# Local attention in two stacked transformer blocks: the exponentials of each block of queries are issued one round behind its scores instead of four blocks at once

## The chip, the cores and the metric

The kernel runs on one core of a Trainium2 chip. The metric is the device time of one execution in microseconds. Three runs of the kernel before took 3441.42, 3444.75 and 3445.19 us, a median of 3444.75. The profiled execution took 3442.09 us.

## The reference

512 tokens of width 1024 pass through two stacks of two layers each, in float32. The parts with local attention are two. The first stack's mixer (once per layer) projects the input to a short convolution, to attention with 8 query heads and 2 key heads of 64, and to a gated 31-tap convolution. The second stack's second layer has attention with 16 query heads and 4 key heads. Around them stand feed-forward parts, a recurrent mixer and cross attention, which the change does not touch.

```python
scores = jnp.where(valid, scores, -1e30)          # 128 queries against 3 (or 2) blocks of 128 keys
m = jnp.maximum(jnp.max(scores, axis=-1), sink)
p = jnp.exp(scores - m[..., None])
denom = jnp.sum(p, axis=-1) + jnp.exp(sink - m)
o = einsum(p, v) / denom
```

## The kernel before, in words

Each engine runs its own program, in order. One Python walk (class `Walk`) is run once for each engine, and each engine's class overrides the `p_...` methods that it takes part in. So the order of the walk is the order of every queue. Waits are semaphore waits for named results.

**Projections.** All large products are computed on TensorE in three passes over a high and a low part. A unit is one block of 128 output columns: its weights are loaded, ScalarE makes the high part (`wh`, L1901), VectorE the low part (`wl`, L2124), up to four units ahead, and TensorE runs 8 steps of three products (L1719, L1720, L1727).

**Fillers.** Attention does not run by itself. It is a generator, and `tick` (called after each step of a projection) takes it one round on for every 2.8 steps in the first mixer and every 2 steps in the second stack's attention, after a delay of 8 and 4 steps. In the first mixer each round also advances the long convolution (`long_conv`: two, later four taps on VectorE, L2299) and the removal of the mean from the residual (`center`, L2173 and L2178). At the end of the projections the rounds that are left run without projection steps between them.

**A round of attention** (`attention`). Round n works on the score of block n of a list of heads times 4 blocks of queries, and on earlier ones with fixed lags:

- norm of block n-5: P times 1/denominator (on ScalarE, L1984, in the first mixer; on VectorE, L2292, in the second attention). For block 0 of a head VectorE first adds the sums and inverts them (L2287, L2289).
- value product of block n-9 on TensorE (L1788). After block 3 the head's output is split: high half on ScalarE (L1907), low half on VectorE (L2128), and only then is its bank free.
- score of block n: product on TensorE (L1773), mask, and row maximum on VectorE (L2275).
- turn of block n-7: transposes on TensorE (L1780), copy on ScalarE (L1991).
- in every fourth round, at its end: `exps` of the head. VectorE makes minus the maximum with the sink for 4 blocks in one operation on 4 columns (L2280). ScalarE waits for it, then computes the sink term (L1976) and the four exponentials in place, each with its row sums (L1978).

**Around it** on ScalarE stand the four part copies of each rope (L1971, VectorE goes on with L2260, L2262 and L2268), the sigmoid of a gate (L1996) and plain copies (L1917). A function of another table set has an ACT_TABLE_LOAD ahead of it; copies need none. In a first mixer rounds 0 and 1 are issued before the first gate's sigmoid; in the second attention rounds 0 and 1 are issued before a rope, and there each unit of weights is followed by four rounds.

Of the kernel before, what the change touches and what calls it, by code (L numbers as in the profile page):

```python
# [10 lines left out]
ALU = mybir.AluOpType  # L11
ACT = mybir.ActivationFunctionType
AX = mybir.AxisListType.X

P = 128
# [3 lines left out]
NB = 4  # L19
# [290 lines left out]
class Walk:  # L310
# [497 lines left out]

    def attention(self, heads, H, blocks, mask, sink, outs, done, on_act=False):
        S, C, PT, obank = {}, {}, {}, {}  # L810
        NORM, TURN, VALUE = 5, 7, 9
        a = self.uid("att")

        def score(h, b):
            q, k, v, tile, p0, qk, vk, n = heads[h]
            k0, nk, c0 = blocks(b)
            if b == 0:
                C[h] = self.sm_ring.take()
            bank, f = self.psum.take()
            s, sf = self.tmp.take()  # L820
            self.p_score(f"{a}.{h}.{b}", bank, s, C[h][0], b, nk * P, q[:, b * P:(b + 1) * P],
                         k[:, k0 * P:(k0 + nk) * P], mask[:, c0:c0 + nk * P], (f, qk), (sf, C[h][1]))
            self.psum.give(bank, f"{a}.{h}.{b}.max")
            S[h, b] = s

        def exps(h):
            tiles = [(S[h, b][:, 0:blocks(b)[1] * P]) for b in range(NB)]
            self.p_exps(f"{a}.{h}", C[h][0], tiles, sink(heads[h][-1]), f"{a}.{h}.{NB - 1}.max")

        def norm(h, b):  # L830
            s = S[h, b]
            self.p_norm(f"{a}.{h}", b, C[h][0], s[:, 0:blocks(b)[1] * P], on_act)
            if b == NB - 1:
                self.sm_ring.give(C[h][0], [f"{a}.{h}.{i}.norm" for i in range(NB)])

        def turn(h, b):
            w = blocks(b)[1] * P
            s = S.pop((h, b))
            bank, f = self.psum.take()
            pt, pf = self.tmp.take()  # L840
            k = f"{a}.{h}.{b}"
            self.p_turn(k, bank, s, pt, w, f, pf)
            self.tmp.give(s, f"{k}.turn")
            self.psum.give(bank, f"{k}.pt")
            PT[h, b] = pt

        def value(h, b):
            q, k, v, tile, p0, qk, vk, n = heads[h]
            k0, nk, c0 = blocks(b)
            pt = PT.pop((h, b))  # L850
            if b == 0:
                obank[h] = self.psum.take()
            bank, f = obank[h]
            key = f"{a}.{h}.{b}"
            self.p_value(key, bank[:, b * P:(b + 1) * P], [v(k0 + i) for i in range(nk)], pt, (f, vk[0][vk[1]]))
            self.tmp.give(pt, f"{key}.value")
            if b == NB - 1:
                self.psum.give(bank, outs(tile, p0, bank, f"{key}.value"))
            done[0] = f"{key}.value"

        for n in range(H * NB + VALUE):
            while n < H * NB and len(heads) <= n // NB:
                yield
            for lag, f in ((NORM, norm), (VALUE, value), (0, score), (TURN, turn)):
                if 0 <= n - lag < H * NB:
                    f(*divmod(n - lag, NB))
            if n < H * NB and n % NB == NB - 1:
                exps(n // NB)
            yield

    def to_hidden(self, tile0):
# [1018 lines left out]
class Scalar(Engine):  # L1890
# [80 lines left out]
            sw = self.e.activation(b_[o:o + 32, :], bank[i:i + 32, :], ACT.Copy)  # L1971
        sw.then_inc(self.s["act"], self.tag("act", f"{k}.sw"))

    def p_exps(self, k, c, tiles, sink, last):
        self.hold.wait_ge(*self.at(f"{k}.m"))
        self.e.activation(c[:, 12:16], c[:, 4:8], ACT.Exp, bias=sink)  # L1976
        for b, s in enumerate(tiles):
            x = self.e.activation(s, s, ACT.Exp, bias=c[:, 4 + b:5 + b], accum_out=c[:, 8 + b:9 + b])  # L1978
        x.then_inc(self.s["act"], self.tag("act", f"{k}.exp"))

    def p_norm(self, k, b, c, s, on_act):
        if on_act:
            self.hold.wait_ge(*self.at(f"{k}.rs"))
            self.e.activation(s, s, ACT.Copy, scale=c[:, 20 + b:21 + b]).then_inc(  # L1984
                self.s["act"], self.tag("act", f"{k}.{b}.norm"))
# [128 lines left out]
class Vector(Engine):  # L2114
# [160 lines left out]
        self.e.tensor_tensor_reduce(s[:, 0:w], bank[:, 0:w], mask, 1.0, -3e38, ALU.add, ALU.max, c[:, b:b + 1]).then_inc(  # L2275
            self.s["dve"], self.tag("dve", f"{key}.max"))

    def p_exps(self, k, c, tiles, sink, last):
        self.hold.wait_ge(*self.at(last))
        self.e.tensor_scalar(c[:, 4:8], c[:, 0:4], sink, -1.0, ALU.max, ALU.mult).then_inc(  # L2280
            self.s["dve"], self.tag("dve", f"{k}.m"))

    def p_norm(self, k, b, c, s, on_act):
        e, hold, dve = self.e, self.hold, self.s["dve"]
        if b == 0:
            hold.wait_ge(*self.at(f"{k}.exp"))
            e.tensor_tensor(c[:, 16:20], c[:, 8:12], c[:, 12:16], ALU.add).then_inc(dve, self.tag("dve", f"{k}.den"))  # L2287
            hold.wait_ge(*self.own("dve"))
            e.reciprocal(c[:, 20:24], c[:, 16:20]).then_inc(dve, self.tag("dve", f"{k}.rs"))  # L2289
        if not on_act:  # L2290
            hold.wait_ge(*self.at(f"{k}.rs"))
            e.tensor_scalar(s, s, c[:, 20 + b:21 + b], None, ALU.mult).then_inc(  # L2292
                dve, self.tag("dve", f"{k}.{b}.norm"))
# [355 lines left out]
```

## Time and profile before

| what | value |
|---|---|
| median of three runs | 3444.75 us |
| profiled execution, its span | 3442.09 us, 3440.3 us |
| TensorE busy | 3354.0 us, 97% |
| VectorE busy | 1781.1 us, 52% |
| ScalarE busy | 1336.5 us, 39% |
| mean granted clock of TensorE | 0.996 of 2.4 GHz |

Engines in the rows: PE is TensorE (PEld its weight loads), DVE is VectorE, ACT is ScalarE, POOL is GpSimd, SP is SyncE. A row of a timeline gives the start in us from the start of the span, the duration in us, the engine, the line, the operation, what it writes and reads, and in brackets how long the engine was idle before it and what ended that. Durations of neighbours overlap a little, so the distance of two starts is what an operation takes from its engine. Names: `wh`, `wl` are weights' high and low part; `HHa`, `HLa` a hidden tile's; `ps` is a PSUM bank; `tmp`, `Y`, `M` hold P and other work tiles; `sm` small columns. First mixers stand at 395 to 540 us and 1344 to 1490 us, the second attention at 2725 to 2890 us.

### The profile page before, as it was taken

The page shows a single profiled execution, that of the slowest core. Times are in us where ns is not written, and L with a number is a line of the kernel's source. Part 1 is how long each engine was busy: PE and PEld are TensorE (multiplying, and loading weights), DVE is VectorE, ACT ScalarE, POOL GpSimd, SP SyncE. Part 2 cuts the span into 40 slices and gives each one's busy share as a digit, 9 for nine tenths or more (in the row PEclk, how much of TensorE's full clock was granted, in tenths as well). Part 3 has the DMA queues.
Part 4 walks back from the last instruction along what each step waited for, and adds up shares of the span by engine and source line. Part 5 has one row for each costly group of instructions (what it writes and reads, how often), then busy time and mean ns, then how long its engine had stood idle before and what let it go on. Part 6 is the DMA issues. An engine that isn't in the chain of part 4 may idle for free.

```text
span 3440.3 us, 38145 instructions
## 1 busy us (share of the span) xinstructions
PE 3354.0 (97%) x15606; PEld 2748.3 (80%) x15606; DVE 1781.1 (52%) x2710; ACT 1336.5 (39%) x2120; POOL 62.7 (2%) x65
## 2 busy tenths in 40 slices
PE   9999989999999999899999999999999989999999
PEld 7888767888888887678888778777888778778887
DVE  4333785533363337855433775647444765655443
ACT  3222554322242225553322554334322565434322
POOL 0000100000000001000000000000000000000000
PEclk9999999999999999999999999999999999999999
DMA  5332311333333333123333333222333313223332
GB/s 158 98 98 88 85 50 56 104 98 98 93 88 100 95 90 87 47 59 104 108 95 93 92 92 105 86 62 77 103 94 98 86 56 98 68 62 104 98 98 68
DMA packets 604286, 304.10 MB, mean 88 GB/s; under 512 B 43600, under 2 KB 601808, under 8 KB 603984
## 3 DMA queue, kind: packets, MB, share of 16 engines
q1 hardware_dynamic: 604112, 301.66, 30.6%
q8 instruction: 124, 2.03, 0.2%
q14 instruction: 50, 0.41, 0.0%
HBM read 299.52 MB, written 2.10 MB: 88 GB/s over the span
## 4 chain that ended last, share of the span: by engine, by line
PE 82%; DVE 10%; ACT 6%; issue 1%; DMA 1%; SPq 0%; DVEq 0%; ACTq 0%
PE ps L1719 25%; PE ps L1720 25%; PE ps L1727 25%; DVE wl L2124 1%; DVE Y L2299 1%; DVE tmp L2133 1%; ACT wh L1901 1%; PE ps L1735 1%; PE ps L1788 1%; PE ps L1886 1%; PE ps L1870 1%; ACT tmp L1971 1%; ACT tmp L1978 1%; PE ps L1773 0%; ACT HHa L1907 0%
## 5 line engine op out<-in xcount | busy, mean ns | idle before, releaser
L1727 PE MATMUL ps<-XL,wh 128*128 128x512 f32 (+1 forms) x2856 | 1061.1, 382 | 0.5 <-DVE XL L2200 0.5
L1719 PE MATMUL ps<-XH,wh 128*128 128x512 f32 (+1 forms) x2624 | 1045.6, 399 | 16.1 <-DVE wl L2124 6.4
L1720 PE MATMUL ps<-XH,wl 128*128 128x512 f32 (+1 forms) x2624 | 1018.4, 389 | 0.0
L2124 DVE TENSOR_TENSOR wl<-raw,wh 128x1024 fp32r<-128x1024 f32 (+1 forms) x565 | 681.5, 1209 | 537.7 <-ACT wh L1901 537.0
L1901 ACT ACTIVATE wh<-raw 128x1024 fp32r<-128x1024 f32 (+1 forms) x565 | 585.4, 1039 | 565.7 <-PE ps L1727 537.0
L1727 PEld LDWEIGHTS ps<-XL,wh 128*128 128x128 f32 x2856 | 537.8, 189 | 104.7 <-DVE XL L2200 1.1
L1719 PEld LDWEIGHTS ps<-XH,wh 128*128 128x128 f32 x2624 | 494.9, 189 | 133.3 <-issue 14.4
L1720 PEld LDWEIGHTS ps<-XH,wl 128*128 128x128 f32 x2624 | 495.1, 189 | 99.7 <-issue 3.1
L1719 PE MATMUL ps<-HHa,wh 128*128 128x512 f32 x1088 | 428.5, 394 | 5.7 <-DVE HLa L2128 5.7
L1720 PE MATMUL ps<-HHa,wl 128*128 128x512 f32 x1088 | 423.9, 390 | 0.0
L1727 PE MATMUL ps<-HLa,wh 128*128 128x512 f32 x1088 | 408.2, 390 | 0.0
L1719 PEld LDWEIGHTS ps<-HHa,wh 128*128 128x128 f32 x1088 | 204.3, 188 | 49.4 <-DVE HLa L2128 7.0
L1727 PEld LDWEIGHTS ps<-HLa,wh 128*128 128x128 f32 x1088 | 204.3, 188 | 42.6
L1720 PEld LDWEIGHTS ps<-HHa,wl 128*128 128x128 f32 x1088 | 204.4, 188 | 41.9 <-issue 0.5
L1727 PE MATMUL ps<-HLb,wh 128*128 128x512 f32 x512 | 199.3, 389 | 0.0
L1719 PE MATMUL ps<-HHb,wh 128*128 128x512 f32 x512 | 199.3, 389 | 0.0
L1720 PE MATMUL ps<-HHb,wl 128*128 128x512 f32 x512 | 199.3, 389 | 0.0
L2227 DVE SCALAR_TENSOR_TENSOR tmp<-tmp,ps 128x512 f32<-128x512 f32 x88 | 60.5, 687 | 210.6 <-PE ps L1727 208.6
L1907 ACT ACTIVATE HHa<-tmp 128x512 fp32r<-128x512 f32 x97 | 61.3, 632 | 255.9 <-DVE tmp L2227 240.7
L1957 ACT ACTIVATE tmp<-ps 128x512 f32<-128x512 f32 x88 | 52.5, 596 | 238.1 <-PE ps L1727 238.0
L2128 DVE TENSOR_TENSOR HLa<-tmp,HHa 128x512 fp32r<-128x512 f32 x97 | 67.2, 693 | 90.7 <-ACT HHa L1907 90.7
L1719 PEld LDWEIGHTS ps<-HHb,wh 128*128 128x128 f32 x512 | 96.1, 188 | 20.0
(331 smaller groups left out, 3072.2 us busy)
## 6 DMA issues: line engine op xcount, KB each, us to landing
raw<-in_ffn_w_gu SPq DMA_DIRECT2D x176, 512.0 KB, 3.8
raw<-in_w_ff SPq DMA_DIRECT2D x128, 512.0 KB, 4.1
raw<-in_ffn_w_down SPq DMA_DIRECT2D x64, 512.0 KB, 4.0
raw<-in_w_xkv SPq DMA_DIRECT2D x32, 512.0 KB, 3.9
raw<-in_ev_w_in SPq DMA_DIRECT2D x25, 512.0 KB, 3.9
raw<-in_ffn_w_down SPq DMA_DIRECT2D x32, 384.0 KB, 3.3
raw<-in_w_in SPq DMA_DIRECT2D x24, 512.0 KB, 3.9
raw<-in_w_out SPq DMA_DIRECT2D x64, 128.0 KB, 2.8
```

Source lines behind the costliest of these rows:

```text
L1719: e.matmul(bank[:, c], t.wh[u % SPL][:, k, :], h[:, c], start=first, stop=False, skip_group_check=True)
L1720: e.matmul(bank[:, c], t.wl[u % SPL][:, k, :], h[:, c], start=False, stop=False, skip_group_check=True)
L1727: m = e.matmul(bank[:, 0:n], t.wh[u % SPL][:, k, :], l, start=False, stop=last, skip_group_check=True)
L1735: m = self.e.matmul(tb[:, b * WIDE:(b + 1) * WIDE], x[:, b * P:(b + 1) * P], self.t.ones[:, 0:WIDE], start=first and b == 0, stop=last, sk ...
L1788: m = self.e.matmul(out, v, pt[:, i * P:(i + 1) * P], start=i == 0, stop=i == len(vs) - 1)
L1870: m = self.e.matmul(bank[:, 0:256], self.t.M0[:, 2 * h + i, b * P:(b + 1) * P], KT[:, 2 * h + i, :], start=i == 0, stop=i == 1)
L1901: self.e.activation(self.t.wh[s][:, 0:nk, :], self.t.raw[r][:, 0:nk, :], ACT.Copy).then_inc(self.s["hi"], self.tag("hi", f"hi.{i}"))
L1907: self.e.activation(hi, src, ACT.Copy).then_inc(self.s["act"], self.tag("act", f"{k}.hi"))
L1957: self.e.activation(q[:, :], gb[:, :], ACT.Silu).then_inc(self.s["act"], self.tag("act", key))
L2124: self.e.tensor_tensor(wl, raw, f32(wh), ALU.subtract).then_inc(self.s["lo"], self.tag("lo", f"lo.{i}"))
L2128: self.e.tensor_tensor(lo, src, f32(hi), ALU.subtract).then_inc(self.s["dve"], self.tag("dve", k))
L2227: self.e.scalar_tensor_tensor(out=h[:, :], in0=q[:, :], scalar=0.5, in1=ub[:, :], op0=ALU.mult, op1=ALU.mult).then_inc(self.s["dve"], self ...
```

## The change

The exponentials get a lag of their own, one round behind the score, and come first in a round. `exps` now handles one block: VectorE's small operation on one column, then ScalarE's exponential of that block; with the last block of a head ScalarE also computes the sink term, from all four columns. The denominator waits for the last block's exponential.

```diff
-        NORM, TURN, VALUE = 5, 7, 9
+        EXPS, NORM, TURN, VALUE = 1, 5, 7, 9
...
-        def exps(h):
-            tiles = [(S[h, b][:, 0:blocks(b)[1] * P]) for b in range(NB)]
-            self.p_exps(f"{a}.{h}", C[h][0], tiles, sink(heads[h][-1]), f"{a}.{h}.{NB - 1}.max")
+        def exps(h, b):
+            self.p_exps(f"{a}.{h}.{b}", b, C[h][0], S[h, b][:, 0:blocks(b)[1] * P], sink(heads[h][-1]))
...
-            for lag, f in ((NORM, norm), (VALUE, value), (0, score), (TURN, turn)):
+            for lag, f in ((EXPS, exps), (NORM, norm), (VALUE, value), (0, score), (TURN, turn)):
                 if 0 <= n - lag < H * NB:
                     f(*divmod(n - lag, NB))
-            if n < H * NB and n % NB == NB - 1:
-                exps(n // NB)
...
-    def p_exps(self, k, c, tiles, sink, last):
+    def p_exps(self, k, b, c, s, sink):
         self.hold.wait_ge(*self.at(f"{k}.m"))
-        self.e.activation(c[:, 12:16], c[:, 4:8], ACT.Exp, bias=sink)
-        for b, s in enumerate(tiles):
-            x = self.e.activation(s, s, ACT.Exp, bias=c[:, 4 + b:5 + b], accum_out=c[:, 8 + b:9 + b])
-        x.then_inc(self.s["act"], self.tag("act", f"{k}.exp"))
+        if b == NB - 1:
+            self.e.activation(c[:, 12:16], c[:, 4:8], ACT.Exp, bias=sink)
+        self.e.activation(s, s, ACT.Exp, bias=c[:, 4 + b:5 + b], accum_out=c[:, 8 + b:9 + b]).then_inc(
+            self.s["act"], self.tag("act", f"{k}.exp"))
...
-    def p_exps(self, k, c, tiles, sink, last):
-        self.hold.wait_ge(*self.at(last))
-        self.e.tensor_scalar(c[:, 4:8], c[:, 0:4], sink, -1.0, ALU.max, ALU.mult).then_inc(
+    def p_exps(self, k, b, c, s, sink):
+        self.hold.wait_ge(*self.at(f"{k}.max"))
+        self.e.tensor_scalar(c[:, 4 + b:5 + b], c[:, b:b + 1], sink, -1.0, ALU.max, ALU.mult).then_inc(
             self.s["dve"], self.tag("dve", f"{k}.m"))
...
         if b == 0:
-            hold.wait_ge(*self.at(f"{k}.exp"))
+            hold.wait_ge(*self.at(f"{k}.{NB - 1}.exp"))
```

## Rows read from the trace of the kernel before

**Rows 1.** The page, parts 1 and 4: busy time by engine, chain that ended last.

```profile
PE 3354.0 (97%) x15606; PEld 2748.3 (80%) x15606; DVE 1781.1 (52%) x2710; ACT 1336.5 (39%) x2120; POOL 62.7 (2%) x65
...
PE 82%; DVE 10%; ACT 6%; issue 1%; DMA 1%; SPq 0%; DVEq 0%; ACTq 0%
```

**Rows 2.** Timeline (start, us, engine, line, operation, [idle before, releaser]): TensorE, mixer.

```profile
502.21 1.13 PE L1788 MATMUL ps<-tmp,M 128*128 128x128 f32 x6 [2.92 <-ACT tmp L1991]
```

**Rows 3.** Timeline of TensorE, second block's attention.

```profile
2774.43 0.44 PE L1780 MATMUL ps<-CT,tmp 128*128 128x128 f32 x2 [1.12 <-DVE tmp L2292]
...
2800.50 1.23 PE L1788 MATMUL ps<-tmp,M 128*128 128x128 f32 x4 [3.41 <-ACT tmp L1991]
```

**Rows 4.** Stretches: busy us by engine, granted clock, DMA share, GB/s.

```profile
460.00:470.00 10.00, 7.24 (x36) 5.86 (x37) 9.90 (x20) 5.67 (x10) 0.00 (x0) 0.93 0.13 37
...
2800.00:2805.00 5.00, 4.50 (x24) 4.11 (x25) 4.44 (x19) 2.39 (x9) 0.00 (x0) 0.66 0.01 3
```

**Rows 5.** Timeline of VectorE, mixer: its stops for ScalarE.

```profile
417.12 1.22 DVE L2124 TENSOR_TENSOR wl<-raw,wh 128x1024 fp32r<-128x1024 f32 x1 [1.36 <-ACT wh L1901]
...
428.98 0.69 DVE L2260 SCALAR_TENSOR_TENSOR M<-ps,CT 128x512 f32<-128x512 f32 x1 [3.54 <-ACT tmp L1971]
...
444.23 0.68 DVE L2128 TENSOR_TENSOR HLa<-ps,HHa 64x512 fp32r<-64x512 f32 x1 [1.58 <-ACT HHa L1907]
...
459.48 0.69 DVE L2128 TENSOR_TENSOR HLa<-ps,HHa 64x512 fp32r<-64x512 f32 x1 [0.36 <-ACT HHa L1907]
...
478.53 1.23 DVE L2124 TENSOR_TENSOR wl<-raw,wh 128x1024 fp32r<-128x1024 f32 x1 [1.37 <-ACT wh L1901]
...
494.88 0.69 DVE L2128 TENSOR_TENSOR HLa<-ps,HHa 64x512 fp32r<-64x512 f32 x1 [2.13 <-ACT HHa L1907]
...
509.62 1.23 DVE L2124 TENSOR_TENSOR wl<-raw,wh 128x1024 fp32r<-128x1024 f32 x1 [2.56 <-ACT wh L1901]
```

**Rows 6.** Waits of the whole kernel (us in total, times, longest).

```profile
ACT sm L1976 <- DVE sm L2280: 72.8, 30, 4.9
```

**Rows 7.** Timeline of VectorE around one small operation, L2280.

```profile
413.27 0.08 DVE L2275 DVE_READ_ACCUMULATOR2_ANT sm<- 128x1 f32 x1
413.39 0.23 DVE L2280 TENSOR_SCALAR sm<-sm,CT 128x4 f32<-128x4 f32 x1
413.52 0.69 DVE L2173 TENSOR_TENSOR tmp<-tmp,XR 128x512 f32<-128x512 f32 x1
```

**Rows 8.** Timeline of ScalarE: exponentials of a head; norm and high half.

```profile
413.65 0.30 ACT L1976 ACTIVATE sm<-sm,CT 128x4 f32<-128x4 f32 x1 [3.26 <-DVE sm L2280]
413.86 0.49 ACT L1978 ACTIVATE tmp<-tmp,sm 128x256 f32<-128x256 f32 x1
...
443.22 0.49 ACT L1984 ACTIVATE M<-M,sm 128x256 f32<-128x256 f32 x1
443.62 0.57 ACT L1907 ACTIVATE HHa<-ps 64x512 fp32r<-64x512 f32 x1
```

**Rows 9.** Timeline of ScalarE at a gate: table load, sigmoid, weights.

```profile
435.90 1.28 ACT L1996 ACT_TABLE_LOAD   x1
437.20 0.60 ACT L1996 ACTIVATE tmp<-ps 128x512 f32<-128x512 f32 x1
437.69 1.05 ACT L1901 ACTIVATE wh<-raw 128x1024 fp32r<-128x1024 f32 x1
```

**Rows 10.** Timeline of VectorE at the mixer's start: second score, weights.

```profile
409.63 0.55 DVE L2275 CUSTOM_DVE_ANT_0 tmp<-ps,CT 128x384 f32<-128x384 f32 x1
...
410.71 1.22 DVE L2124 TENSOR_TENSOR wl<-raw,wh 128x1024 fp32r<-128x1024 f32 x1
```

**Rows 11.** Timeline of ScalarE, second block's attention: rope's part copies, P's copies.

```profile
2728.18 2.39 ACT L1971 ACTIVATE Y<-ps 32x512 f32<-32x512 f32 x4
...
2771.24 0.55 ACT L1991 ACTIVATE tmp<-ps 128x256 f32<-128x256 f32 x2
```

**Rows 12.** Timeline of VectorE, second block's attention: its second score.

```profile
2731.25 0.42 DVE L2275 CUSTOM_DVE_ANT_0 Y<-ps,CT 128x256 f32<-128x256 f32 x1
```

## The prediction

> **What bounds the kernel now.** I read the head of the page first: TensorE is busy 97% of the span and makes 82% of the chain that ended last [rows 1]. The reader sees there that time can only come from the pauses of TensorE. The diff adds or moves nothing on TensorE, so its queue keeps its order, and what can change is when its waits end. So I next read its timeline, and noted each instruction with an idle time ahead of it, in the three stretches that run local attention: twice the first mixer (402 to 540 us, and the same pattern 949 us later), and once the second block's attention (2725 to 2890 us).
>
> In a first mixer eight pauses of over 0.9 us make 13.8 us, the longest for ScalarE's copy of a turned P (L1991), 2.92 us [rows 2]; others for VectorE's low half of an attention output (L2128). In the second block's attention twelve pauses of over 0.3 us make 14.9 us, all before 2809 us. Two kinds [rows 3]: about 1.1 us once per unit of weights, for the norm on VectorE (L2292), and 3.41 us (later 2.44) for the copy L1991. Behind the pause of 3.41 us TensorE's granted clock is 0.66 over 5 us [rows 4], a mean between its levels of 2.4 and 1.2 GHz: 5 x 0.34 = 1.7 us lost.
>
> Who is late? In 460 to 470 us VectorE is busy 9.90 of 10 us, ScalarE 5.67 [rows 4]. In the mixer VectorE sets the pace: it runs the 31-tap convolution's four taps per round behind attention's work. It stops almost only for ScalarE, seven times between 410 and 510 us [rows 5]. All seven have the row of four exponentials ahead of what they wait for on ScalarE. That is what the change attacks. Against that stands ScalarE's own long idle time before each row, 72.8 us over 30 heads, for the small operation L2280 [rows 6]: ScalarE has room.
>
> **The change part by part.** Terms are lateness against the profiled execution; a queue is followed in its order, with the durations of the rows. The queues of SP and POOL and their transfers keep their order too; a weight load waits for its buffer, and none was late in these stretches.
>
> *Small operations.* L2280 runs 32 times now and 128 times after. One lasts 0.23 us, but the next operation starts 0.13 us behind it [rows 7], so I count 0.14. Now a head pays 0.14, and about 0.12 for waiting on the score just ahead of it (413.27 to 413.39). After, it pays 4 x 0.14 and mostly no such wait: 4 x 0.14 - 0.26, about +0.31 us of VectorE per head, +0.17 where its last one stands at the start of a wait that I count separately. The Trainium skill (VectorE: DVE Perf Modes, "The TRN2 errata") says that each instruction from SBUF pays a fixed latency between instructions, small ones in full. By that a small operation would cost its whole 0.23 us, and the two mixers 16 x 3 x 0.09 = 4.3 us more. The trace's start to start of 0.13 us speaks against it here.
>
> *The wait that comes.* The small operation and the exponential for the last block of a head now stand at the start of round 4h+4 on both engines. Head h's last value product comes in round 4h+12, where also head h+2's last exponential is due, so both meet the split of head h's output. VectorE's order in it: small operation, low half, score, then taps. ScalarE's: sink term, exponential, norm, high half, copy. So from the small operation to the low half pass 0.26 (413.39 to 413.65) + 0.21 (to 413.86) + 0.49 (exponential) + 0.40 (norm, 443.22 to 443.62) + 0.61 (high half, to 444.23) = 1.97 us [rows 5, 7, 8]. Nothing covers it: the taps of the previous round, which now run while ScalarE works off the row of exponentials, stand ahead of the small operation after the change. Queued behind VectorE's low half are the score, the taps and the next weights' low half, and TensorE waits for them. In exchange the present stops shrink.
>
> *First gate of a mixer.* Rounds 0 and 1 are issued before the first sigmoid, so the first exponential comes ahead of it on ScalarE, and waits for the small operation that VectorE reaches at 409.63 [rows 10]. ScalarE then: exponential 409.89 to 410.38, table load 1.28, sigmoid 0.49, wh 1.05: 413.20, where wl began at 410.71 now [rows 9, 10]. That is 2.5 us on VectorE, and one more table load per mixer (five loads for exponentials over the kernel become seven). The Trainium skill (ScalarE: Activation LUTs, "What ACT_TABLE_LOAD costs") gives 1283 ns for the load and about 1380 ns of drain. In the trace the sigmoid at 437.20 starts 1.30 us after the load at 435.90 does [rows 9], without such a drain, so the load alone counts; by the rule the two mixers would be 2.8 us later. Of the 2.5 us most returns: the stop at 417.12 (1.36) shrinks to about 0.3, that at 428.98 (3.54) to about 1.6, since four part copies of rope there no longer wait behind a whole row. With the small operations 0.5 us is left at round 8.
>
> *Sum for one mixer* at the low halves: round 12, 0.5 + 0.31 + (1.97 - 1.58) = 1.2. Round 16, + 0.17 + (1.97 - 0.36) = 3.0. Round 20, the 1.37 for wl goes and 1.97 comes: + 0.17 + 0.60 = 3.75. Round 24, + 0.17 + (1.97 - 2.13) = 3.8. Round 28, the 2.56 for wl shrinks to about 1.3: + 0.17 + 0.71 = 4.6 [rows 5]. VectorE waits a little for TensorE behind that (0.3 + 0.35), of which I give back 0.3: 4.3 us at the convolution's column sums, for which TensorE waits. TensorE cannot hide it, as it is already at most two rounds ahead: a value product needs the copy of two rounds before. Bounds: 0 if TensorE's slack holds it all, and below zero, -4, if the stops of rows 5 go (12.9 us) and only half of the 5 x 1.97 come; above, 4.3 plus two falls of the clock of 1.7 us: 8. I take 4.3, since the walk runs row by row and VectorE was at 9.90 of 10 us in the middle of it. Two mixers: +8.6.
>
> *Second block's attention.* Here the norm is on VectorE and no taps run. At its start the first exponential comes ahead of the four part copies of a query's rope, now 2728.18 to 2730.57; it waits for the small operation at 2731.25, so they end at 2731.25 + 0.26 + 0.39 + 2.39 = 2734.3, 2.7 us later than VectorE's rope now begins [rows 11, 12]. VectorE's first two waits for the sum of exponentials, 3.8 us together, shrink by some 1.8: +0.9. Then per unit of weights (four rounds, four of them): three exponentials leave the chain from the small operation to the high half, which gives 1.37 (0.39 + 2 x 0.49). But the copies at 2771.24 [rows 11], now free, stand behind exponentials that wait for a small operation behind the weights' low half, at about 2774.0, and the rope's part copies stand behind the next head's first. Walked through, the period is 11.6 instead of 11.1 us: 4 x 0.5 = +2.0. In the rounds without weights (2797 to 2809) the shorter chain takes 1.4 us off each of two pauses and probably spares the clock's fall: -4.4. From 2809 TensorE is the bound with other work: 0. Sum -1.5; I take -1. Bounds: -8 (all 1.1 us pauses gone too), +6 (no gain in the tail, and a fall of the clock).
>
> **Total.** 8.6 - 1 = +7.6. The profiled execution took 3442.1 us (span 3440.3 and 1.8 around it), so 3449.7; it lies 2.7 below the median of 3444.75, for which I add the same: 3452.4. I say 3453.
>
> **Rivals.**
> *A, ScalarE free early wins (faster).* If VectorE is not more than a round behind TensorE, the small operations find their score ready, three of four exponentials run in ScalarE's idle time, and every pause behind a row of them shrinks by about 1.4 us: four in each mixer, seven in the second attention, 15 x 1.4 = 21, less 5 for the small operations: 3429 to 3434; I put it at 3431. For: the 72.8 us of idle time, the second attention's tail. Against: VectorE reaches the second score at 409.63 [rows 10], over 4 us after TensorE had it done, and stays full behind it. It decides at the point where VectorE's round starts before TensorE's value product of the next.
> *B, nothing (same).* The new stops fall where VectorE stops now, and cancel: the small operations only, 32 x 0.1: 3447. For: the present seven stops sum to 12.9 us, close to the new ones (five of 1.97 and 2.5).
> *C, the clock too.* The forecast's mechanism, and the pauses grow long enough for two more falls of the clock at 1.7 us in each of the three stretches: 3453 + 10 = 3463. For: the fall behind 3.41 us [rows 4]. Against: more pauses of 2 us, as I forecast them, need not be such.
>
> **How the numbers follow.** Forecast 0.50 (3447 to 3460), A 0.15, B 0.25, C 0.10. No change is within 0.2%, or 6.9 us, of 3444.75. Slower by more: most of the forecast (0.40), C, a bit of B: 0.52. Same: 0.31. Faster: 0.17. The range is 3436 to 3465; it leaves out most of A and half of C.
>
> **What would show it.** Right: low halves at the rounds where a head's last exponential is due with waits of 1.5 to 2 us in VectorE's rows, five per mixer; wl near 413 instead of 410.7 us; seven table loads; a longer first mixer by 3 to 6 us, equal in both layers; the second attention within 3 us of now. Wrong: VectorE stopping less in the mixer than now, or pauses of TensorE before L1788 gone; then A holds.

## The result, and the profile after

The changed kernel takes 3461.11 us, the median of four runs (3457.84 to 3462.81), beside 3444.61 us for the kernel before on the same chip: ratio 1.0049, 95% interval 1.0038 to 1.0061. It is 16.5 us slower. The forecast was 3453, slower by 8.3 than the median then known, half of that; the range (3436 to 3465) holds the result, the band that I gave the forecast itself (3447 to 3460) does not. Its profiled execution took 3462.81 us with a span of 3461.0, so the two profiles lie 20.7 us apart.

The page after, parts 1 and 4, beside [rows 1]:

```profile
PE 3367.6 (97%) x15606; PEld 2757.7 (80%) x15606; DVE 1793.8 (52%) x2806; ACT 1343.6 (39%) x2122; POOL 62.7 (2%) x65
...
PE 80%; DVE 12%; ACT 6%; issue 1%; DMA 0%; SPq 0%; DVEq 0%; ACTq 0%
```

VectorE has 96 operations more, the small ones. TensorE has the same 15606 matmuls and is busy 13.6 us longer: a slower clock. That looks like two thirds of the loss. It is not: most of it lies in stretches where TensorE waits for VectorE anyway (experiment 7), and only what falls at the end of a mixer counts, 1.2 us in each (the table at experiments 7 and 8). VectorE's share of the chain rises from 10 to 12%.

To see where the time goes I mark the places that both kernels have: a mixer's first score, the second of the late products behind it (0.42 us of wait for a low half), and the second attention's first score. TensorE's timeline before:

```profile
402.74 0.46 PE L1773 MATMUL ps<-M 128*128 128x256 f32 x1 [0.39 <-DVE M L2268]
...
541.79 0.50 PE L1719 MATMUL ps<-HHa,wh 128*128 128x512 f32 x1 [0.42 <-DVE HLa L2128]
...
2725.45 0.35 PE L1773 MATMUL ps<-M 128*128 128x128 f32 x1 [0.49 <-DVE M L2268]
```

and after (its lines stand 2 to 4 lower in the code):

```profile
402.18 0.45 PE L1770 MATMUL ps<-M 128*128 128x256 f32 x1 [0.39 <-DVE M L2265]
...
548.32 0.50 PE L1716 MATMUL ps<-HHa,wh 128*128 128x512 f32 x1 [0.43 <-DVE HLa L2125]
...
2741.95 0.35 PE L1770 MATMUL ps<-M 128*128 128x128 f32 x1 [0.50 <-DVE M L2265]
```

The first mixer takes 139.05 us before and 146.14 after. The same marks, read in the profiles of the experiments below as well, in us (the last column runs to the end of the span; between the mixers lie 809.7 in all of them, and between the second mixer and the second attention 1235.9 to 1238.2):

| kernel | mixer 1 | mixer 2 | from the second attention on |
|---|---|---|---|
| before | 139.05 | 137.48 | 714.85 |
| after | 146.14 | 146.15 | 719.05 |
| the change in the mixers alone | 146.16 | 146.16 | 714.96 |
| the change in the second attention alone | 139.06 | 139.06 | 719.20 |
| idle small ops added | 142.49 | 142.48 | 717.98 |
| exponential at the end of its own round | 139.26 | 139.28 | 736.26 |
| exponential at the end of the next round | 132.61 | 132.64 | 708.81 |
| the same, small op a round earlier | 135.85 | 135.79 | 708.17 |
| as after, the last block's exponential late | 138.02 | 136.69 | 713.57 |
| as after, the first exponential late | 142.04 | 140.41 | 718.85 |
| as before, the row issued one round later | 132.85 | 132.83 | 705.45 |
| as after, pauses filled | 147.03 | 146.13 | 719.10 |
| as before, pauses filled | 136.69 | 138.29 | 714.73 |

Before's own second mixer (137.48) is 1.6 short of its first, by the clock at its end (the table at experiments 7 and 8); the profiles of the second attention alone and of the extra table load, in which the mixers' order is that of before, have 139.06 to 139.15 in all four mixers. So the change costs about 7.1 us in each mixer and 4.2 us from the second attention on.

VectorE's stops for ScalarE in the first mixer after, beside [rows 5]; the last number in brackets is the idle time:

```profile
412.81 1.23 DVE L2121 TENSOR_TENSOR wl<-raw,wh 128x1024 fp32r<-128x1024 f32 x1 [2.45 <-ACT wh L1898]
...
418.23 1.23 DVE L2121 TENSOR_TENSOR wl<-raw,wh 128x1024 fp32r<-128x1024 f32 x1 [0.26 <-ACT wh L1898]
...
428.85 0.69 DVE L2257 SCALAR_TENSOR_TENSOR M<-ps,CT 128x512 f32<-128x512 f32 x1 [2.19 <-ACT tmp L1968]
...
440.72 1.22 DVE L2121 TENSOR_TENSOR wl<-raw,wh 128x1024 fp32r<-128x1024 f32 x1 [1.89 <-ACT wh L1898]
...
446.32 0.68 DVE L2125 TENSOR_TENSOR HLa<-ps,HHa 64x512 fp32r<-64x512 f32 x1 [1.74 <-ACT HHa L1904]
...
463.31 0.69 DVE L2125 TENSOR_TENSOR HLa<-ps,HHa 64x512 fp32r<-64x512 f32 x1 [1.87 <-ACT HHa L1904]
...
484.21 0.68 DVE L2125 TENSOR_TENSOR HLa<-ps,HHa 64x512 fp32r<-64x512 f32 x1 [1.73 <-ACT HHa L1904]
...
499.41 0.69 DVE L2125 TENSOR_TENSOR HLa<-ps,HHa 64x512 fp32r<-64x512 f32 x1 [1.87 <-ACT HHa L1904]
...
516.00 0.68 DVE L2125 TENSOR_TENSOR HLa<-ps,HHa 64x512 fp32r<-64x512 f32 x1 [1.74 <-ACT HHa L1904]
```

Five low halves (rounds 12 to 28) each stand 1.7 to 1.9 us, as forecast. One of them close up, on ScalarE and on VectorE:

```profile
461.47 0.30 ACT L1974 ACTIVATE sm<-sm,CT 128x4 f32<-128x4 f32 x1 [2.19 <-DVE sm L2277]
461.68 0.49 ACT L1975 ACTIVATE Y<-Y,sm 128x256 f32<-128x256 f32 x1
...
462.17 0.49 ACT L1981 ACTIVATE tmp<-tmp,sm 128x256 f32<-128x256 f32 x1
462.68 0.59 ACT L1904 ACTIVATE HHa<-ps 64x512 fp32r<-64x512 f32 x1
```

```profile
460.64 0.68 DVE L2175 SCALAR_TENSOR_TENSOR XR<-ps,XR 128x512 f32<-128x512 f32 x1
461.24 0.20 DVE L2277 TENSOR_SCALAR sm<-sm,CT 128x1 f32<-128x1 f32 x1
```

ScalarE idles 2.19 us for a small operation that VectorE reaches behind its taps; the norm and the high half, whose inputs have long been there, stand behind it in ScalarE's queue; then VectorE idles for the high half. Each engine waits for the other once.

### The profile page after: what moved, and what is told of

It is laid out like the page before. It is cut to its first block, busy times and chain, and to the rows that moved or that the text cites. A ratio compares the mean times of both kernels' runs of the same rounds, so it can differ in the third digit from the quotient of the medians.

```text
span 3461.0 us, 38243 instructions
## 1 busy us (share of the span) xinstructions
PE 3367.6 (97%) x15606; PEld 2757.7 (80%) x15606; DVE 1793.8 (52%) x2806; ACT 1343.6 (39%) x2122; POOL 62.7 (2%) x65
## 4 chain that ended last, share of the span: by engine, by line
PE 80%; DVE 12%; ACT 6%; issue 1%; DMA 0%; SPq 0%; DVEq 0%; ACTq 0%
PE ps L1716 25%; PE ps L1717 25%; PE ps L1724 25%; DVE Y L2296 2%; DVE wl L2121 2%; ACT wh L1898 2%; DVE tmp L2130 1%; PE ps L1732 1%; PE ps L1883 1%; PE ps L1867 1%; ACT tmp L1968 1%; PE ps L1785 1%; ACT HHa L1904 0%; DVE HLa L2125 0%; ACT tmp L1975 0%
```

## The experiments

What I set out to show: the loss is the waits that the new order makes (the last exponential stands a round later, behind VectorE's taps; exponentials ahead of the gates' sigmoids) and falls of the clock. The rivals: the small operations by themselves, the table loads, the clock alone. A time is the median of 5 to 11 executions, a ratio is to the kernel before on the same chip (15 to 23 executions), and "more" or "less" without another name is against that. Medians of two experiments can come from two chips, on which the kernel before has 3443.19 to 3444.61. The diffs give in short form the calls in one round of `attention`, where `(lag, step)` works on block n - lag: `base` is norm, value product, score and turn, `small` the small operation on VectorE, `exp1` the exponential on ScalarE.

**1 and 2. The change in one place each.**

```diff
+ steps = ((1, small), (1, exp1)) + base     # mixers alone / second attention alone
```

> The change in the first stack's mixer alone (both layers), the second attention as before. My theory (the last block's exponential of a head, now at the start of a round behind VectorE's taps, and the first exponentials ahead of the gates' sigmoids, stop VectorE where nothing covers it) puts most of the loss here: +10 to +16 us against before. A rival, that the loss is spread by the number of blocks (64 in the two mixers, 64 in the second attention), gives +8.

> The change in the second block's attention alone. My theory: +1 to +6 us (the start of it 1.4 to 1.9 us late, some 0.5 us per unit of weights, 1 to 3 us back in the rounds without weights, and falls of the clock behind the longer pauses). My prediction had -1. The rival that counts blocks: +8. If ScalarE free early wins here: -3 or less.

Mixers alone: 3459.88 us, ratio 1.0046 (1.0033 to 1.0059), 16 us more. Second attention alone: 3447.56, 1.0012 (1.0003 to 1.0021), 3.8 us more. The loss is mostly in the mixers; the second attention, forecast at -1, loses 4 as well. The two profiles add up: each part is as long as in the changed kernel where the change is in, and as before where it is not.

**3. The small operations alone.** The kernel before with the three more small operations of each head at the start of the rounds, their results not used otherwise.

```diff
+ if 0 < n <= H * NB and n % NB: small(*divmod(n - 1, NB))
```

> The kernel before, with three of the change's one-column operations on VectorE added per head at the starts of rounds (96 in all); nobody waits for them, and the row of four exponentials stays as it was. It tells the operations' own cost from the waits. My theory: 48 of them in the mixers at 0.14 us, partly in idle time: +2 to +5 us. The rival that the added operations are the change's cost: +14 or more. If each costs its whole duration of 0.21 us: up to +10.

3453.41 us, ratio 1.0028 (1.0017 to 1.0039): 9.6 us more, over the 2 to 5 that I expected. A mixer grows by 3.4 us, the rest by 3.1. The low halves tell how. Measured from the first score, the one at round 12 is 0.85 us later than before, and those at rounds 16, 20, 24 and 28 are 1.21, 1.58, 1.95 and 2.31: a steady 0.36 per head, 0.12 per added operation. That is the distance of two starts in [rows 7], and VectorE pays it every time, since it has no idle time that would absorb it. This is more than the change itself pays: here the four-column operation of each head is still there, with its wait for the row maximum just ahead. Another 1.1 us comes at the end of the mixer, where TensorE pauses 3.05 us and then runs slowly:

```profile
525.00:530.00 5.00, 5.00 (x17) 4.18 (x17) 0.00 (x0) 0.04 (x1) 0.00 (x0) 0.53 0.02 5
```

TensorE is busy 5.00 of 5 us with VectorE and ScalarE done, at a granted clock of 0.53: here its clock is on the path (the table at experiments 7 and 8).

**4. One more table load per mixer**, by an exponential of one column ahead of each gate's sigmoid. Only the first gate of a mixer gets a load more by it: ScalarE has 2126 instructions for 2120, four exponentials and two loads.

```diff
+ e.activation(sm[:, 124:125], ones[:, 0:1], ACT.Exp)     # ahead of the sigmoid
```

> The kernel before, with one exponential of a single column ahead of each gate's sigmoid in the mixers, not waiting for VectorE. At the first gate of a mixer that brings one more table load, as in the change, without the change's wait. My theory: the loads lie in ScalarE's idle time, 0 to +1 us. The rival that a switch of tables costs its time on the path: +3 (two loads) to +5.5 (with a drain of 1.4 us each).

3444.34 us, ratio 1.0001 (0.9993 to 1.001). Loads that ScalarE can do while it would wait cost nothing. The load that the change itself adds comes behind a late exponential, and is another matter (experiment 9).

**5 and 6. The same instructions, other places in the round.**

```diff
+ steps = base + ((0, small), (0, exp1))          # 5: end of the own round
+ steps = ((1, small),) + base + ((1, exp1),)     # 6: exponential at the next round's end
```

> Both attentions: the small op and the exponential of a block stand at the end of the block's own round, behind its row maximum, instead of at the start of the next. Same instructions as the changed kernel, one per block. The earlier run with three idle small ops per head took +9.6 us over the kernel before, with the exponentials left in a row. Theory (what is left of the loss, some 7 us, comes from the last exponential standing a round later and behind the small op that VectorE reaches late): that part goes, and the time falls to 3446 to 3455, about the run with the idle small ops alone. Rival 1 (ScalarE coupled to VectorE in every round costs the same wherever in the round it stands): 3457 to 3464. Rival 2 (the extra table loads ahead of the gates' sigmoids make the loss): the loads stay, 3457 or more.

> Both attentions: the small op of a block at the start of the next round, as in the changed kernel, but its exponential at the end of that round on ScalarE, behind the round's copies of turned tiles. Theory (the place of the last exponential counts: the norm of a head's first block, four rounds behind its last exponential's block, waits for it): later still than the changed kernel, 3462 to 3475. Rival 1 (what costs are the small ops on VectorE alone, wherever the exponentials stand): 3451 to 3456, as in the run with the idle small ops. Rival 2 (ScalarE standing at the small op at the start of each round is the loss, and by the end of the round the small op is done): 3446 to 3456.

Both theories fell. The end of the own round: 3467.22 us, ratio 1.007 (1.0057 to 1.0083). It is above rival 1's range; rival 2's "3457 or more" holds the number but not the cause, since the loss is in the second attention, where no gate's sigmoid stands. The end of the next round: 3425.51, ratio 0.995 (0.9937 to 0.9964), faster than both kernels with the changed kernel's very instructions. Rival 2 had the mechanism, and even its range ended 20 us above. In its mixer the five low halves have no stop. One of them, on ScalarE and on VectorE:

```profile
456.04 0.59 ACT L1924 ACTIVATE HHa<-ps 64x512 fp32r<-64x512 f32 x1
456.66 0.49 ACT L2015 ACTIVATE tmp<-ps 128x384 f32<-128x384 f32 x1
458.58 0.30 ACT L2001 ACTIVATE sm<-sm,CT 128x4 f32<-128x4 f32 x1 [1.43 <-DVE sm L2309]
458.78 0.49 ACT L2002 ACTIVATE Y<-Y,sm 128x256 f32<-128x256 f32 x1
```

```profile
458.35 0.20 DVE L2309 TENSOR_SCALAR sm<-sm,CT 128x1 f32<-128x1 f32 x1
458.58 0.69 DVE L2152 TENSOR_TENSOR HLa<-ps,HHa 64x512 fp32r<-64x512 f32 x1
```

ScalarE still waits 1.43 us for the small operation, but by then the high half, begun at 456.04, is done, and VectorE's low half at 458.58 has no wait ahead of it. My theory had expected the first norm of the head to suffer, as only the start of the next round stands between; it does not show up.

In the own round's version the mixers are as long as before (139.3; the low half of round 12 is 2.4 us late and that of round 28 only 0.1), and the second attention takes 21 us more. A piece of it at 2850 us, VectorE, ScalarE and TensorE:

```profile
2850.85 0.21 DVE L2309 TENSOR_SCALAR sm<-sm,CT 128x1 f32<-128x1 f32 x1
2852.84 1.23 DVE L2148 TENSOR_TENSOR wl<-raw,wh 128x1024 fp32r<-128x1024 f32 x1 [1.78 <-ACT wh L1918]
...
2855.05 0.21 DVE L2309 TENSOR_SCALAR sm<-sm,CT 128x1 f32<-128x1 f32 x1
```

```profile
2851.10 0.40 ACT L2002 ACTIVATE Y<-Y,sm 128x128 f32<-128x128 f32 x1 [0.94 <-DVE sm L2309]
...
2851.76 1.05 ACT L1918 ACTIVATE wh<-raw 128x1024 fp32r<-128x1024 f32 x1
```

```profile
2855.16 0.30 PE L1797 MATMUL ps<-CT,tmp 128*128 128x128 f32 x1 [0.88 <-DVE sm L2299]
```

The exponential waits for the small operation, the weights' high half behind it waits too, VectorE waits for that high half, and so the next row maximum and small operation come late; TensorE, which between 2809 and 2890 us had only two pauses before, of 0.36 and 0.21 us, stands 0.4 to 0.9 us nearly every second round. It is the same mutual wait, in each round.

**7 and 8. The clock.** Matmuls on a constant tile, with results that are overwritten, ahead of the wait of two value products in each mixer and one in the second attention.

```diff
+ for _ in range(fill): e.matmul(out, ident, ident, start=True, stop=True)
  hold.wait_ge(...)                               # the turned P
```

> The changed kernel with matmuls on a constant tile, whose results are overwritten, placed ahead of the wait at three value products: 18 at 433.9 us of the first mixer's place and 20 at 495.2 us (the same in the second mixer), 30 at 2818.6 us. TensorE then works where it paused 2.8, 3.3 and 4.8 us, and nothing else moves. Theory (over half of what the change costs comes through the slower clock behind such pauses; each of five falls costs some 1.7 us): 3451 to 3459, at least 2 below the changed kernel of the same chip. Rival (the clock follows something else, or the filled pauses only hand the fall to the next pause): within 1.5 us of the changed kernel, 3459.5 to 3463, or slower where the matmuls run past the wait.

> The kernel before with the same idle matmuls at its own longest pauses at value products: 15 ahead of 468.3 us and 18 ahead of 502.2 us in the first mixer (the same in the second), 22 ahead of 2800.5 us. Pauses of 2.5, 2.9 and 3.4 us are filled. Theory (the clock falls behind these pauses and each fall costs up to 1.7 us): 3436 to 3442, faster than before by 2 to 8 us, and so faster than both kernels. Rival (falls that another pause takes over, or matmuls that run past the wait and delay the value product): 3443 to 3447.

Changed kernel filled: 3462.06 us, ratio 1.0056 (1.0044 to 1.0069), no gain. Kernel before filled: 3441.88, ratio 0.9998 (0.999 to 1.0007), no difference that can be measured; the median lies in the theory's range, the interval decides nothing. The stretches of the changed kernel, then of its filled version (us of the stretch, busy PE, PEld, DVE, ACT, POOL, granted clock, DMA share, GB/s):

```profile
435.00:440.00 5.00, 5.00 (x20) 3.71 (x19) 3.76 (x8) 4.05 (x9) 0.00 (x0) 0.68 0.04 12
...
530.00:535.00 5.00, 5.00 (x19) 4.24 (x18) 0.69 (x1) 1.31 (x3) 0.00 (x0) 0.63 0.00 0
...
1358.00:1504.00 146.00, 128.00 (x619) 101.65 (x619) 112.43 (x247) 86.45 (x185) 0.00 (x0) 0.94 0.20 55
```

```profile
435.00:440.00 5.00, 5.00 (x33) 4.27 (x32) 4.25 (x10) 4.05 (x9) 0.00 (x0) 1.00 0.14 42
...
530.00:535.00 5.00, 5.00 (x16) 4.13 (x16) 0.00 (x0) 0.14 (x1) 0.00 (x0) 0.50 0.00 0
...
1358.00:1504.00 146.00, 133.16 (x693) 107.65 (x692) 113.19 (x248) 86.54 (x184) 0.00 (x0) 0.96 0.20 55
```

The filling works: the clock at 435 us goes from 0.68 to 1.00. But the fall at the end of the mixer grew in mixer 1 (0.50 for 0.63), and mixer 2, whose mean clock went from 0.94 to 0.96 (146 x 0.02 = 2.9 us), is 146.13 us long for 146.15. In the middle of the mixer VectorE sets the pace, and a slower TensorE only shortens its own pauses: in both filled kernels VectorE's low halves of rounds 12 to 28 stand within 0.03 us of where they stood without filling, measured from the first score.

Behind the low half of round 28 VectorE runs out of work, and there the clock is on the path. The piece from that low half to the next one, by the granted clock:

| kernel, mixer | piece, us | clock |
|---|---|---|
| before, 1 and 2 | 17.07, 15.50 | 0.90, 1.00 |
| before with pauses filled, 1 and 2 | 14.72, 16.30 | 1.00, 0.90 |
| the first exponential late (experiment 9), 1 and 2 | 16.77, 15.20 | 0.90, 1.00 |
| after, 1 and 2 | 18.27, 18.37 | 0.81, 0.81 |
| after with pauses filled, 1 and 2 | 19.09, 18.31 | 0.73, 0.81 |

In the first three rows the two mixers of one execution differ only here (by 0.04 us at most at round 28), each time by 1.6 us, and that is what a mean clock of 0.90 in place of 1.00 costs. At 0.81 the changed kernel is 3.1 us over the 15.20 of experiment 9, and 1.2 us over before's first mixer. The filled pauses lie ahead of this piece, and in the filled changed kernel its clock is no higher. So experiment 7 clears the clock in the middle of the mixers, not at their end.

In the second attention the filling does not settle much. The matmuls ran past the wait: from the first score to the filled value product pass 78.09 us for 76.69 in the changed kernel, and 76.43 for 75.05 before. The clock behind it was 1.00 for 0.59 (0.66 before), and the stage ends where it did, 719.10 for 719.05 and 714.73 for 714.85: the clock may have given back what the delay cost; the two are not separated.

**9. The first exponential out of the first gate's way.**

```diff
+ # mixers: small(0, 0) and exp1(0, 0) in round 2, not in round 1
```

> The changed kernel, but in the mixers the very first exponential, with its small op, goes from the start of round 1 to the start of round 2, out of the way of the first gate's sigmoid. Prediction: the first gate's 2.5 us mostly come back by round 8, so little is won: 0 to 1 us a mixer, 3458 to 3461. Theory after the traces (the second gate, 1.7 us late, keeps what the first lost): the second gate is late by another head's exponential and stays so, 3456 to 3461; the mixer takes 145 to 146 us. Rival (the gates make the loss): the mixer falls under 144 us, 3454 to 3457.

3452.78 us, ratio 1.0029 (1.0018 to 1.0041), 8.3 less than the changed kernel (about 7 by the ratios; the two profiles come from opposite ends of their kernels' runs and lie 11.3 apart): a mixer is 4.1 and 5.7 us shorter. The forecast's view of this place and my view after the traces both missed; the rival held, and even its range ended 1.2 us above. Two rows of VectorE:

```profile
438.67 1.23 DVE L2154 TENSOR_TENSOR wl<-raw,wh 128x1024 fp32r<-128x1024 f32 x1 [1.90 <-ACT wh L1924]
...
444.27 0.68 DVE L2158 TENSOR_TENSOR HLa<-ps,HHa 64x512 fp32r<-64x512 f32 x1 [1.74 <-ACT HHa L1930]
```

From its first score (402.65) to this low half of round 12 pass 41.62 us, after the change 446.32 - 402.18 = 44.14: the whole 2.5 us of the first gate were still there at round 12 (the table load that the late exponential had added, 1.28 us, is in them). The second gate's stop of 1.90 stays, but this low half is only 0.13 us later than before's (444.23 - 402.74 = 41.49): that stop is paid by what the change saves up to there. I had blamed it, and it does not count. The 2.5 us stay up to round 28; the other 1.6 and 3.2 us of the two mixers come behind it, where the clock is 0.90 and 1.00 for 0.81.

**10. The last block's exponential alone at the end of the round.**

```diff
+ steps = ((1, small), (1, exp1 if b < 3)) + base + ((1, exp1 if b == 3),)
```

> Both attentions: as the changed kernel, but the exponential of a head's last block alone goes from the start of the next round to its end on ScalarE, behind the split's high half and the round's copies; the other three stay at the start, and all small ops stay. The changed kernel's mixer takes 146.15 us, the one with all four exponentials at the end 132.6. Theory (VectorE's low half of a head's output waits 1.7 to 1.9 us, five times a mixer, for a high half that stands behind the last exponential; 5 x 1.8 = 9): the mixer falls to 136 to 139 us and the five stops are gone; with some in the second attention, 3438 to 3448. Rival (all four exponentials at the start of a round cost alike, as ScalarE there waits each time for VectorE's small op): a quarter of 13.5, 142 to 144 us a mixer, 3452 to 3458.

3438.58 us, ratio 0.999 (0.9981 to 0.9999). As the theory had it: mixers 138.0 and 136.7, four of the five stops gone and the fifth at 0.65 us.

```profile
459.84 0.69 DVE L2169 TENSOR_TENSOR HLa<-ps,HHa 64x512 fp32r<-64x512 f32 x1
...
492.89 0.69 DVE L2169 TENSOR_TENSOR HLa<-ps,HHa 64x512 fp32r<-64x512 f32 x1 [0.65 <-ACT HHa L1939]
```

One call in four, moved from one end of a round to the other, is worth 22.5 us between the two medians, about 20 by the ratios (in the profiles 8.1 and 9.5 in the mixers, 5.5 in the second attention).

**11. The row of four, one round later on ScalarE.** The kernel before, small operation in its place; only ScalarE's row moves behind the next round's copies.

```diff
- if n < H * NB and n % NB == NB - 1: exps(n // NB)
+ if n < H * NB and n % NB == NB - 1: exps(n // NB, vector part)
+ if 0 < n <= H * NB and n % NB == 0: exps(n // NB - 1, scalar part)
```

> Both attentions: the kernel before, with one small op a head where it was, and its row of four exponentials in a row, but the row issued one round later on ScalarE: at the end of round 4h+4, behind that round's norm, high half and copies, instead of ahead of them. No instruction is added. Theory (what counts is only which copies stand behind the exponentials in ScalarE's queue): faster than before, and without the extra small ops (3.4 us a mixer by the run with the idle ones) about as good as one exponential at the end of each round: 3420 to 3436. Rival (the row of 2.4 us is then directly ahead of the sum and norm of round 4h+5, so VectorE and ScalarE stand there; spreading is what pays): 3440 to 3455.

3422.82 us (3421.15 to 3423.14), ratio 0.9938 (0.9926 to 0.9951): the fastest of all, 21 us below before and 38 below the changed kernel, with no instruction added. ScalarE and VectorE at a low half:

```profile
450.35 0.59 ACT L1939 ACTIVATE HHa<-ps 64x512 fp32r<-64x512 f32 x1 [1.74 <-PE ps L1820]
451.11 0.49 ACT L2032 ACTIVATE tmp<-ps 128x384 f32<-128x384 f32 x1 [0.17 <-PE ps L1812]
451.50 0.29 ACT L2010 ACTIVATE sm<-sm,CT 128x4 f32<-128x4 f32 x1
```

```profile
454.28 0.69 DVE L2169 TENSOR_TENSOR HLa<-ps,HHa 64x512 fp32r<-64x512 f32 x1
```

The high half is done at 450.94, 3.3 us before VectorE wants it, and the row runs from 451.50 to 454 under VectorE's taps, without a wait for the small operation. Spreading the exponentials over the rounds was never needed: what the row cost was the copies queued behind it.

**12. The small operation right behind its row maximum**, exponential as in 6.

```diff
+ steps = base + ((0, small), (1, exp1))
```

> Both attentions: exponential of a block at the end of the next round on ScalarE, as in the fast arrangement (3425.5 us), but its small op right behind its row maximum, at the end of VectorE's own round, so that ScalarE never waits for it (it now waits 31 times in a mixer and in the second attention, up to 0.8 to 1.0 us). Theory (those waits are on the path in the second attention, where weights' high half stands behind them): 3415 to 3424. Rival (the small op has to wait for the maximum just ahead of it, about 0.12 us for each of 128, on the engine that sets the pace): 3425 to 3435.

3429.74 us, ratio 0.9957 (0.9944 to 0.9969), 4 us above experiment 6, as the rival had it. The second attention gains 0.6 us, and a mixer loses 3.2. The number is that of the rival, 32 waits of 0.10 us for the maximum just ahead, but the loss does not build up so. At round 12 the low half is 1.6 us earlier than in experiment 6; by round 28 the waits (16 x 0.10) have used that up, 102.27 for 102.23 us from the first score. All 3.2 us come behind it, in a piece of 18.94 us at a clock of 0.91 for 15.74 at 1.00. Why TensorE enters it with more left to do I have not taken apart.

## Why the prediction was right, and what it mis-sized

Direction, place and mechanism held; the size was 16.5 us against about 8. Of the signs named, the five waits, wl near 413 us and seven table loads for exponentials came; a mixer longer by 3 to 6 us (it is 7.1, equal in both layers) and the second attention within 3 us (it is 4.2) did not. Between the profiles a mixer is 2.8 us over its 4.3: 1.4 at the first gate, 1.6 at the end, -0.2 between. The second attention is 5.2 us over its -1, most of it in its rounds without weights.

**What bounds it.** Right. VectorE sets the pace in the mixers, and all that was seen there up to round 28 follows from its queue; experiment 7 confirms it from the other side. Behind round 28 TensorE's clock has a part in it, which the sum left out. The reading of the second attention's pauses was short by one: 0.36 us at 2865 us, behind the 2809 named.

**Small operations: right in the mixers, left out in the second attention.** The 0.14 us each was nearly right (0.12 to 0.13 from start to start). The credit for the wait on the score held in the mixers: none of the 32 small operations of the changed kernel's first mixer stands right behind the read of a maximum, while before all eight did and started 0.12 us behind it, where operations that need not wait start 0.00 behind it. Experiment 3 shows 0.36 per head, not 0.31 and 0.17, because it leaves the four-column operation and its wait in place; it is no measure of the forecast's term. In the second attention, where no taps stand between, 33 of the 64 small operations do stand right behind the maximum and start 0.12 us late; the sum had nothing for them. Experiment 3 shows 3.1 us there, as an upper bound; what they cost in the changed kernel is not measured apart. From the rule of the Trainium skill (VectorE: DVE Perf Modes, "The TRN2 errata"; a fixed latency between instructions, small ones in full) I read that an operation costs its whole duration, 0.2 us; the steady 0.12 per operation in experiment 3 speaks against that reading. An estimate by the table of the same section (58 cycles plus the elements, at 0.96 GHz) is 0.06 us, and the trace has twice that.

**The wait that comes.** Right: 1.97 us forecast from the small operation to the low half, 463.31 - 461.24 = 2.07 in the trace, and 1.94 to 2.08 at the five rounds named. Experiment 10 shows that this wait alone outweighs all that the change gains.

**First gate.** The wait was right (wl forecast at 413.20, seen at 412.81 with a start 0.56 earlier; the stop at 417.12 down to 0.26; rope's down to 2.19 for 1.6). The step "of the 2.5 us most returns" failed: 2.5 remain at round 12 and up to round 28, and are gone without it (experiment 9; the mixer is 4 to 6 us shorter there, the rest by the clock at its end). I also missed a stop of 1.89 us at the second gate, which as it turned out costs nothing net. There exponential, norm and copy stand ahead of the sigmoid:

```profile
436.35 0.62 ACT L1975 ACTIVATE tmp<-tmp,sm 128x384 f32<-128x384 f32 x1 [0.92 <-DVE sm L2277]
...
437.85 1.28 ACT L1993 ACT_TABLE_LOAD   x1
439.15 0.60 ACT L1993 ACTIVATE tmp<-ps 128x512 f32<-128x512 f32 x1
```

The sigmoid ran at 437.20 before [rows 9]. From load to sigmoid pass 1.30 us here too. The Trainium skill's drain of about 1380 ns at a change of tables (ScalarE: Activation LUTs, "What ACT_TABLE_LOAD costs") is again not to be seen.

**Lateness at the low halves**, from the first score: forecast 1.2, 3.0, 3.75, 3.8, 4.6; measured 2.65, 4.4, 5.1, 5.1, 5.8. The walk's increments behind round 12 are right to 0.1 us; the nearly constant 1.2 to 1.45 is what the first gate left.

**The end of the mixer.** I gave back 0.3; instead 1.2 to 1.3 us more are lost between round 28 and the end. There TensorE pauses 2.69 us and its clock is 0.63 to 0.69. In experiment 3 a like piece is 1.1 us. The piece behind round 28 is 18.3 us at a clock of 0.81 after, 17.07 at 0.90 before; there the clock is on the path (the table at experiments 7 and 8), and the lower clock accounts for this piece. The sum had falls of the clock only in its upper bound. What makes the clock fall there is not shown.

**Second attention.** Forecast -1, measured +4.2. The start was right: 2.63 us of stop at the rope for 2.7. By VectorE's low halves of weights, from the first score, it is 1.3 us late at the fourth (forecast 0.9) and 3.8 at the seventh, ahead of the rounds without weights (forecast 2.9). The pause at the start and the one in those rounds:

```profile
2757.71 0.33 PE L1777 MATMUL ps<-CT,tmp 128*128 128x128 f32 x1 [2.37 <-DVE tmp L2289]
...
2818.64 0.58 PE L1785 MATMUL ps<-Y,M 128*128 128x128 f32 x1 [4.80 <-ACT Y L1988]
```

and what ScalarE did ahead of the copy that the second one waits for:

```profile
2817.57 0.51 ACT L1975 ACTIVATE tmp<-tmp,sm 128x256 f32<-128x256 f32 x1 [2.56 <-DVE sm L2277]
...
2818.20 0.38 ACT L1988 ACTIVATE Y<-ps 128x256 f32<-128x256 f32 x1
```

The rounds without weights, forecast to win 4.4 us by a shorter chain, are the term that failed: they have a pause of 4.80 us, ahead of block 3 of head 4, where the longest was 3.41, ahead of block 1 of head 5 [rows 3]; behind it the clock is 0.59 over 5 us, and the next low half of weights is 4.75 us late, so nothing was won. It is the mutual wait once more: VectorE stood 2.61 us for the rope's part copies, so its small operation came at 2817.33; ScalarE's exponential waited 2.56 us for that, and the copy that TensorE waited for stood behind it. Here it is the exponential of an earlier block of its head: experiment 10, which moves only the last, takes 5.5 us off this stage and still has the pause of 4.80; in experiment 6, with all four moved, no pause of TensorE in this stage is over 2.37.

**Rivals.** A (ScalarE free early) would have been right for the same instructions in another place: experiment 6 is at 3425. B fell: the new stops do not cancel the old. C named 3463 and is near the number, mostly by luck: of the falls that it adds, only what comes at the end of each mixer is shown on the path (1.2 us each over before's first mixer); filling those in the middle bought nothing back. The rest of what C adds is matched by the first gate and by the second attention.

## What to carry to other kernels

When engines run in-order queues, ask of each instruction that may wait what stands behind it, not only what stands ahead: put it behind everything in its round whose inputs are ready, and, where there is a choice, late enough that what it needs is ready. Experiment 5 shows why the second part belongs to it: at the end of its own round the exponential waits for a maximum just computed, with the next weights' high half behind it, and that was the slowest kernel of all. Here that place was worth more than the number of instructions or their grouping, and it was free. On the engine that sets the pace, each added instruction costs its start-to-start distance, however small it is, and a gap is not there to absorb it unless the profile shows one. Before a slower clock is blamed, check whether TensorE was waiting for others in that stretch anyway; and before it is cleared, check the stretches where the others have run out of work.

## What was not expected of the hardware

TensorE's busy time rose by 13.6 us with the same matmuls, yet filling two pauses in each mixer, with the mean clock of the second up from 0.94 to 0.96, shortened neither. The stretch that counts lies behind both. And a fall that was filled came back elsewhere: in the filled mixer 1 the stretch at 530 us ran at 0.50, for 0.63 without the filling. Two mixers of the same order differ by up to 1.6 us in one execution (139.05 and 137.48 before; 142.04 and 140.41 in experiment 9), with a mean granted clock of 0.96 and 0.98 before. Before, VectorE's low halves up to round 28 agree in both to 0.01 us, and TensorE pauses 1.67 us behind it in both, and yet the clock of that piece is 0.90 in one and 1.00 in the other. What brings it down stays open.
